# Two transformer blocks with sixteen experts: the expert weights' high parts through a ring of three buffers, down products in three passes, one-hots spread over the experts, router on rows before their norm

## The reference, cut to what matters

```python
x = x + gt1 * (concat([att, conv]) @ w_out)                  # 1024 x 1024
h = modulate(rmsnorm_2(x, g_ffn), sh2, sc2)                  # x/rms * g * (1+sc2) + sh2
aff = jax.nn.softmax(h @ w_router, axis=-1)                  # 16 experts
g, idx = lax.top_k(jnp.swapaxes(aff, 1, 2), 128)             # 128 tokens for each expert
xs = h[idx]
a = jnp.einsum('becd,edf->becf', xs, w_gate)                 # 1024 x 1024 for each expert
u = jnp.einsum('becd,edf->becf', xs, w_up)
y = jnp.einsum('becf,efd->becd', jax.nn.silu(a) * u, w_down) * g[..., None]
x = x + gt2 * segment_sum(y, idx)
return rmsnorm_2(x, g_final)
```

## Time and profile before

| | us |
|---|---|
| median of three runs | 2641.08 (2640.81 to 2642.41) |
| the profiled execution, its own time | 2639.82 |
| its span | 2638.2 |
| PE busy | 2503.8 (95%) |
| DVE busy | 1466.5 (56%) |
| ACT busy | 932.5 (35%) |
| POOL busy | 202.0 (8%) |

### The profile page before, as it was taken

One profiled execution on the slowest core, in us unless ns is written; L12 is line 12 of the kernel. 1 busy time (PEld: TensorE's weight loads), 2 busy tenths in 40 slices (PEclk: granted clock), 3 DMA queues, 4 the chain that ended last, 5 costly groups with the idle time before them and its releaser, 6 DMA issues.

```text
span 2638.2 us, 29916 instructions
## 1 busy us (share of the span) xinstructions
PE 2503.8 (95%) x11800; PEld 1970.0 (75%) x11800; DVE 1466.5 (56%) x1936; ACT 932.5 (35%) x1492; POOL 202.0 (8%) x224
## 2 busy tenths in 40 slices
PE   7999899999999999999999999999976999999996
PEld 6787578878888787788878888776865776667663
DVE  6999745224343564445445933576458655655562
ACT  4233524334231122112123421555262544544452
POOL 1001310000000000010000100000021001101100
PEclk9999989999999999999999999999977999999998
...
GB/s 146 64 41 44 32 96 65 97 96 9 32 57 68 84 112 80 99 84 114 87 112 32 151 49 17 64 1 26 112 244 203 340 357 366 370 369 364 361 355 218
DMA packets 116404, 370.53 MB, mean 140 GB/s; under 512 B 6309, under 2 KB 15701, under 8 KB 116304
## 3 DMA queue, kind: packets, MB, share of 16 engines
...
## 4 chain that ended last, share of the span: by engine, by line
PE 84%; DVE 10%; ACT 3%; issue 1%; DMA 1%; POOL 1%; SPq 0%; ACTq 0%; DVEq 0%; POOLq 0%
PE banks L431 22%; PE banks L433 21%; PE banks L432 21%; PE banks L2483 8%; DVE conv_out L1433 4%; DVE w_lo L425 2%; PE banks L2359 2%; PE banks L531 1%; PE banks L2407 1%; PE banks L2226 1%; PE banks L2205 1%; ACT w_hi L418 1%; DVE one_hot L1929 1%; PE banks L2376 1%; PE banks L2377 1%
## 5 line engine op out<-in xcount | busy, mean ns | idle before, releaser
L1979 DVE TENSOR_TENSOR expert_w_lo<-expert_w,expert_w_hi 128x2048 fp32r<-128x2048 f32 x120 | 269.0, 2285 | 212.2 <-ACT expert_w_hi L1318 212.0
L431 PE MATMUL banks<-act_hi,w_hi 128*128 128x512 f32 x960 | 376.8, 393 | 7.2 <-DVE w_lo L425 4.1
L433 PE MATMUL banks<-act_hi,w_lo 128*128 128x512 f32 x960 | 374.6, 390 | 0.0
L432 PE MATMUL banks<-act_lo,w_hi 128*128 128x512 f32 x960 | 374.5, 390 | 0.0
L1318 ACT ACTIVATE expert_w_hi<-expert_w 128x2048 fp32r<-128x2048 f32 x128 | 237.5, 1905 | 127.7 <-DMA expert_w<-in_w_gate 80.9
L418 ACT ACTIVATE w_hi<-w_raw 128x1024 fp32r<-128x1024 f32 x152 | 156.9, 1060 | 297.4 <-PE banks L433 297.3
L425 DVE TENSOR_TENSOR w_lo<-w_raw,w_hi 128x1024 fp32r<-128x1024 f32 x152 | 181.6, 1222 | 140.5 <-ACT w_hi L418 136.1
L431 PE MATMUL banks<-w_hi,act_hi 128*128 128x512 f32 (+1 forms) x640 | 245.8, 384 | 6.6 <-DVE w_lo L425 2.9
L433 PE MATMUL banks<-w_hi,act_lo 128*128 128x512 f32 (+1 forms) x640 | 243.1, 380 | 0.0
L432 PE MATMUL banks<-w_lo,act_hi 128*128 128x512 f32 (+1 forms) x640 | 242.8, 379 | 0.0
L431 PEld LDWEIGHTS banks<-act_hi,w_hi 128*128 128x128 f32 x960 | 180.9, 188 | 47.8 <-issue 4.2
...
## 6 DMA issues: line engine op xcount, KB each, us to landing
expert_w<-in_w_gate SPq DMA_DIRECT2D x32, 2048.0 KB, 9.9
expert_w<-in_w_up SPq DMA_DIRECT2D x32, 2048.0 KB, 10.1
expert_w<-in_w_down SPq DMA_DIRECT2D x32, 2048.0 KB, 8.4
ada_w<-in_w_ada POOLq DMA_DIRECT2D x48, 512.0 KB, 4.2
...
w_raw<-in_w_in SPq DMA_DIRECT2D x18, 512.0 KB, 6.2
```

The source lines that it names most:

```text
L431: nc.tensor.matmul(o_, lh, rh, start=start, stop=False)
L432: nc.tensor.matmul(o_, lh, rl, start=False, stop=False)
L433: return nc.tensor.matmul(o_, ll, rh, start=False, stop=stop)
L1979: dve.tensor_tensor(EWL[slot][:, c, :], EW[slot][:, c, :], EWH[slot][:, c, :], ALU.subtract).then_inc(w_ready, 1)
```

## The change

- **High parts.** EWH has three buffers (*ring*) instead of four, and every piece n of all experts, twelve for an expert, takes the next third of it: ACT may make the high part of piece n when PE has used piece n-6 (`ex_p`, counted by PE after each piece).
- **Down products** have three passes as gate and up have (`split_product` with `HTH`, `HTL`): ACT and DVE convert two slots more for each expert, and DVE makes the low part of the hidden rows. EWL has six members, in the places of the raw slots. SP frees slots by `ex_p`, in the same order as before but for the last expert, whose down weights go to slots 0 and 1.
- **One-hots** of experts 4 to 7 come after the low parts of up(0); those of 8 to 15 go in ones and twos beside experts 1 to 4, and `chosen` runs for four experts at a time. The first five loop turns are written out for it.
- **Router.** PE transposes the rows before their norm (`rows_x3_T`) in the middle of the next tile's product, the router weights are multiplied by gain and scale once (`WRG`), the shift's share is a row of its own (`RBI`, eight products), and DVE multiplies the sums by the token's factor (`RLG`). The normed rows are still made for the gathers; those of tile 7 only after the chosen masks, and their store stands between POOL's low pieces.
- **`turn_over`**: matmuls of no use to the result, 15 among the first four `chosen_of`, and 10 after the first `rows_T`.
- **The end.** The last expert's up product goes by halves of columns, its hidden rows are transposed and converted by halves, and the patched rows are made between the others (`last_rows`).

```diff
-    OHB = at("one_hot", [P, 6, NT, CAP], BF16, O_R + 52 * K + 512)
+    OHB = at("one_hot", [P, 4, NT, CAP], BF16, O_R + 52 * K + 512)
-    EWH = [at(f"expert_w_hi{i}", [P, 4, D], F32R, a) for i, a in enumerate((O_RAW, O_R + 32 * K + 512, O_R + 64 * K + 512, O_R + 4 * K))]
-    EWL = [at(f"expert_w_lo{i}", [P, 4, D], F32R, O_WH + 16 * K * i) for i in range(4)]
+    EWH = [at(f"expert_w_hi{i}", [P, 4, D], F32R, a) for i, a in enumerate((O_RAW, O_R + 32 * K + 512, O_R + 64 * K + 512))]
+    EWL = [at(f"expert_w_lo{i}", [P, 4, D], F32R, O_WH + 16 * K * i) for i in range(6)]
+    OHP = at("one_hot_later", [P, 6, NT, CAP], BF16, O_R + 4 * K)
...
@@ SP @@
-            with sp.Fori(2, NE) as e:
+            with sp.Fori(2, LASTE) as e:
                 for m in range(2):
                     for half in range(2):
-                        load_expert(e, m, half, when=e)
+                        load_expert(e, m, half, used=12 * (e - 2) + (8 + 4 * m + 2 * half + 2))
                 for half in range(2):
-                    load_expert(e - 1, 2, half, when=e - 1)
+                    load_expert(e - 1, 2, half, used=12 * (e - 2) + (16 + 2 * half + 2))
...
@@ POOL @@
             for n in range(POOL_LO):
+                if n == 2:
+                    h2_store(NT - 1)
                 slot, c = n // 2, slice(2 * (n % 2), 2 * (n % 2) + 2)
                 pool.wait_ge(w_hi, W_SPLIT + n + 1)
                 pool.tensor_tensor(EWL[slot][:, c, :], EW[slot][:, c, :], EWH[slot][:, c, :], ALU.subtract).then_inc(w_ready, 1)
...
@@ ACT @@
+            def w_piece_hi(n, slot, j, ring, e):
+                if j == 0:
+                    act.wait_ge(ew_in[slot], 16 * e + 32)
+                if not isinstance(n, int) or n >= 6:
+                    act.wait_ge(ex_p, n - 5)
+                act.activation(EWH[ring][:, 2 * j:2 * j + 2, :], EW[slot][:, 2 * j:2 * j + 2, :], ACT.Copy).then_inc(w_hi, 1)
...
+            for n in range(2):
+                w_piece_hi(n, 0, n, 0, 0)
             for n in range(2):
                 act.wait_ge(h2_out[n], 16 * (NT // 2))
+            for n in range(2):
+                w_piece_hi(2 + n, 1, n, 1, 0)
...
@@ DVE @@
+            def expert_dve(e, first=False, hots=(), sums=None):
+                n = 12 * (e - 1) + 8
+                if not first:
+                    w_piece_lo(n + 4, 2, 0, 0)
+                    w_piece_lo(n + 5, 2, 1, 0)
+                expert_hidden_lo(e - 1)
+                w_piece_lo(n + 6, 3, 0, 1)
+                w_piece_lo(n + 7, 3, 1, 1)
+                w_piece_lo(n + 8, 4, 0, 2)
+                w_piece_lo(n + 9, 4, 1, 2)
+                w_piece_lo(n + 10, 5, 0, 0)
+                for c in hots[:1]:
+                    one_hot(c)
+                w_piece_lo(n + 11, 5, 1, 0)
+                if sums is not None:
+                    chosen(sums, sums + 4, 4)
+                w_piece_lo(n + 12, 0, 0, 1)
+                expert_hidden(e, n + 8)
+                w_piece_lo(n + 13, 0, 1, 1)
+                expert_rows_lo(e + 1)
+                w_piece_lo(n + 14, 1, 0, 2)
+                w_piece_lo(n + 15, 1, 1, 2)
+                for c in hots[1:]:
+                    one_hot(c)
+                expert_y(e, n + 12, first)
...
@@ PE @@
+            def rows_x3_T(t):
+                pe.wait_ge(x3_new, t + 1)
+                for hb in range(2):
+                    q = 2 * (N_EXP + t) + hb
+                    pe.wait_ge(nm_hi, q - 1)
+                    for c in range(4):
+                        k = 4 * hb + c
+                        m = pe.transpose(BK[4 + q % 2][:, c * P:(c + 1) * P], X[:, t, k * P:(k + 1) * P], IDN)
+                    m.then_inc(nm_tp, 1)
...
-            gemm_tokens(B_W2 + 1, T_W2 + 8, after=route)
-            for t in range(NT, NT + 2):
-                route(t)
+            gemm_tokens(B_W2 + 1, T_W2 + 8, middle=lambda t: rows_x3_T(t - 1) if t >= 1 else None,
+                        after=lambda t: router(t - 1) if t >= 1 else None)
+            rows_x3_T(NT - 1)
+            router(NT - 1)
...
             for e in range(4):
                 chosen_of(e)
+                turn_over(6 if e == 0 else 3)
...
+            def expert_pe(e, sums=None):
+                n = 12 * (e - 1) + 8
+                pe.wait_ge(ex_xl, e + 1)
+                pe.wait_ge(ex_sg, e)
+                split_product(0, 0, (1, 2), n)
+                if sums is not None:
+                    pe.wait_ge(ex_y, e)
+                    for c in range(sums, sums + 4):
+                        chosen_of(c)
+                pe.wait_ge(ex_he, e)
+                split_product(1, 2, (0, 1), n + 4)
+                if sums is not None:
+                    pe.wait_ge(tk_out, sums // 4 + 2)
+                pe.wait_ge(ex_hl, e)
+                rows_T(e + 1)
+                pe.wait_ge(ex_y, e)
+                split_product(2, 4, (2, 0), n + 8, HTH, HTL)
                 hidden_T(e, e + 2)
```

534 lines of the change are left out of this document (328 added, 206 removed).

## The result

The changed kernel takes 2592.37 us at the median (2589.14 to 2595.11, four runs), the kernel before 2640.94 (2635.75 to 2642.41). The ratio is 0.9817, with a 95% interval of 0.9805 to 0.9829: 1.8% faster. The forecast was 2591, its range 2574 to 2611. The profiled execution took 2590.50 us over a span of 2588.8, 49.4 less than the span before.

What follows compares the result with a forecast made beforehand. PE was taken to bound the expert loop, with the DMA weight stream nearly as full. Terms: 42.3 - 8.6 + 13.5 + 1 + 2 = 50.2 us less, giving 2591 us, range 2574 to 2611.

Steps and rivals of the forecast that it cites:

- rival 1: Expert loop: PE stays the bound to the end, the weight stream costs nothing; 2579 us, chance 0.22.
- B: Expert loop: the weight stream needs 35.8 us a turn against PE's 34.47, so PE stands 8.6 us in all.
- D: Router and selection, up to gate(0): shorter router, later gather; about +1 us gain, bounds -5 to +7.
- C: One-hots and first experts: gate(0) to gate(1) 11.5 us shorter, plus 2 for gate(1) starting warm; 13.5, bounds 9 to 15.
- the last stretch: From the transposes of expert 15's rows to the end: forecast gain 5.6 us from two down products, 2 from the end.
- A: Down products of experts 0 to 14: each from 13.73 to 10.91 us, 42.3 us less if nothing else holds PE.
- The 35.8: Expert loop: microseconds the weight stream was taken to need in a turn, out of 35.5 to 36.4.
- the 415 GB/s: Expert loop: average rate that full DMA queues must exceed for PE to stay the bound to the end.
- the 2618 us drawn from the derate: Whole kernel: time if the weight stream ran at 368 GB/s, making a loop turn 37.1 us.
- E: The end, after the loop: shorter last product, but scatter and sums' load on the path; +2 us, bounds 0 to 5.
- the later turns of 35 to 36.5 us: Expert loop, sign of the forecast: turns of 34.5 us in experts 2 to 6, later ones 35 to 36.5.
- the 2 us around 1992: Selection, sign of the forecast: first gather goes out within 2 us of 1992, behind a POOL piece that ended just then.

Runs made afterwards that it cites:

- high parts only: Against the changed kernel, down products of experts 0 to 14 leave out passes with low parts, and DVE makes 16 of 1024 columns of their low parts: 2580.13 us.
- the experiment: Against the changed kernel, the one-hots of experts 4 to 15 and their `chosen_of` go back to one stretch, between gate(0) and up(0) on PE: 2602.36 us.
- the two other edits: Against the changed kernel with up(15) loaded before down(14): down(15) loaded after down(14) landed, and ACT's third high part of up(15) before silu; all three edits 2591.60 us.

## Why the prediction was right

The time was met within 2 us, and much of that is luck: errors of both signs cancel. What happened is rival 1, PE as the bound to the end, at the forecast's time. Against the 50.2 us forecast, B's loss of 8.6 did not come; D gave 5.6 less, C 4.7 less and the last stretch 1.3 less; 2.2 came from the scatter ahead of the change: 50.2 + 8.6 - 5.6 - 4.7 - 1.3 + 2.2 = 49.4.

- **A, right, 2 to 3 us too large.** A product gives 2.81 us (2.82 forecast). The last two gave half of it: "if nothing else holds PE" did not hold at the end.
- **B, wrong size.** No wait for the stream came in the loop; the chain that it would take was the right one, shown with high parts only. The step that failed is "the time that the DMA engines need if they never stand idle is 37.27 us less the hole". It took a share of 0.98 to 1.07 for an engine with nothing to spare; but windows of 250 and 426 GB/s had the same share, and the share says that packets are under way, not that more can't be moved. (The 35.8 was also called "nearer to the row", whose 0.83 us would give 36.4; it lies nearer to the other bound.) The need is the bytes by the rate that a full stretch holds: 13.6 MB at 396 to 397 GB/s, 34.3 us. Rival 1's case, then, with no margin to speak of, and without the 415 GB/s that it asked for: 13.64 MB in 34.47 us are 396. The Trainium skill (DMA: Bandwidth & Descriptors, Specifications) gives about 358 GB/s as the limit of HBM for a core, half of what two share, and 368 as the vendor's derate. The trace, with 396 over a whole turn and one core at work, is over both, and the 2618 us drawn from the derate fell with it.
- **C, 4.7 us too large.** Forecast 13.5, measured 8.8 in the trace (10.8 less the 2.0 of `chosen_of` in turns 3 and 5) and 9 to 10 by the experiment. From gate(0) to gate(1) it was 0.7 under the 11.5. The eight later `chosen_of` weren't counted on PE (2.0). And the 2 us for a gate(1) that "after only 1.2 us of idle time may not" begin cold did not come: it was 2.15 us, and the clock fell, as it did in eight of ten such traces.
- **D, 5.6 us too small a loss.** Forecast +1, measured -4.6 (-2.6 + 9.3 - 11.2, rounded). The router gave 9.3 (8.2 forecast). The stretch of the product was to stay (-1.7 + 1.7) and got 2.6 longer: the norm's wait of 1.7 went, but the shift's products take 1.8, and where the rest went is not traced. The gather came 11.3 us later against the affinities, not 7.3. The line store, ACT, POOL, gather was 11.4 us behind the rows, the upper end of its bounds (0.9 over the 10.5 in their middle). What no step had is DVE's copy behind POOL's subtraction, 3.2 us: the prediction asked how POOL is slowed by DVE, not the reverse. `turn_over` did bring gate(0) in at full clock, but it also set its start: the rows' low part was ready 1.5 us earlier (2002.45 + 1.22).
- **E, about right.** Its two products and it were to give 7.6 us and gave 6.3. That SP's issue order holds up(15) back was not seen; alone it is worth nothing (83.2 against 83.6 us), since down(14) then comes late, and with the two other edits about 2 us.
- Of the signs named beforehand, the later turns of 35 to 36.5 us did not come: from the sixth on all are 34.46, which was rival 1's sign. The gather went out behind a POOL piece that had just ended, as named, but at 1994.68, outside the 2 us around 1992. Gate(0) began at full clock, gate(0) to gate(1) was 26.6 (26), and the affinities came 8.0 us after the product (9).
